# Turning the second product of a PEER expert layer: 32 sparse tokens move to the v side, gates come eight blocks at a time

## What is computed

```
s1, s2 = scores of the query halves against 128 keys each     # per token and head (8 heads)
idx, sc = the 16 best of the 128 x 128 pairs                  # expert number, score
gate = softmax(sc)
act  = gelu(u_table[idx] . h)                                 # u_table: 16384 x 1024
y    = sum over heads and experts of gate * act * v_table[idx]
```

## Time and profile before

| | us |
|---|---|
| median of 3 runs | 1489.33 (1485.82 to 1491.83) |
| profiled execution, its own time | 1488.56 |
| its span, first to last instruction | 1486.4 |
| start of the first product (chain of work) | 373.5 |
| start of `main` | 647 |
| start of `POST` | 923.5 |
| start of the second product | 960.2 |

### The profile page before, as it was taken

The page is one execution under the profiler, slowest core; times in us unless marked ns, Lnnn a source line. Parts: engine busy times, 40 slices in busy tenths (PEclk is TensorE's granted clock), DMA queues, the critical chain, the costliest instruction groups (busy, mean ns, idle before and its releaser), DMA issues.

```text
span 1486.4 us, 23381 instructions
## 1 busy us (share of the span) xinstructions
PE 1458.1 (98%) x8069; PEld 1301.4 (88%) x8069; DVE 1165.9 (78%) x2372; ACT 640.8 (43%) x1055; POOL 681.1 (46%) x394
## 2 busy tenths in 40 slices
PE   7999899999999999999999999999999999999998
PEld 6879668888999999999999999888888888888887
DVE  4747563388989999988998888578788778878876
ACT  4463472321433333467777666433332243233221
POOL 2423171233777768865545453134334434433341
PEclk9999999999999999999999999999999999999999
DMA  7400211312689999999999999699999999999993
GB/s 265 149 29 1 113 45 32 114 58 71 192 296 330 317 332 354 417 356 363 371 376 362 356 368 389 218 392 383 379 355 343 354 348 352 346 348 349 354 344 121
DMA packets 183962, 410.29 MB, mean 276 GB/s; under 512 B 12852, under 2 KB 108852, under 8 KB 182360
## 3 DMA queue, kind: packets, MB, share of 16 engines
q1 hardware_dynamic: 142296, 258.46, 49.3%
q0 software_dynamic: 41600, 151.03, 26.9%
HBM read 361.12 MB, written 48.30 MB: 275 GB/s over the span
## 4 chain that ended last, share of the span: by engine, by line
PE 75%; DVE 9%; DMA 9%; POOL 4%; issue 2%; ACT 1%; SPq 0%; DVEq 0%; ACTq 0%; POOLq 0%
PE banks L1996 17%; PE banks L1764 16%; PE banks L2065 12%; PE banks L2064 12%; PE banks L2066 12%; DMA u_rows<-in_u,idx 8%; DVE gate_rows L1623 3%; POOL u_lo L746 3%; DVE u_rows L1568 2%; POOL u_rows L762 2%; DVE u_lo L1551 1%; PE banks L1976 1%; DVE oh L1619 1%; PE banks L1791 1%; PE banks L1836 1%
## 5 line engine op out<-in xcount | busy, mean ns | idle before, releaser
L794 POOL DMA_INDIRECT v_rows<-in_v,idx x128 | 204.2, 1595 | 325.2 <-DVE x_res L1707 273.6
L2064 PE MATMUL banks<-v_hi,w_hi 128*128 128x512 f32 x768 | 298.8, 389 | 0.0
L2066 PE MATMUL banks<-v_hi,w_lo 128*128 128x512 f32 x768 | 298.8, 389 | 0.0
L2065 PE MATMUL banks<-v_lo,w_hi 128*128 128x512 f32 x768 | 298.8, 389 | 0.0
L1125 ACT ACTIVATE v_hi<-v_raw 128x1024 fp32r<-128x1024 f32 x128 | 126.3, 1050 | 326.1 <-PE banks L2066 298.5
L762 POOL DMA_INDIRECT u_rows<-in_u,idx x160 | 189.8, 1186 | 138.7 <-DVE z L1568 107.4
L1645 DVE TENSOR_TENSOR v_lo<-v_raw,v_hi 128x1024 fp32r<-128x1024 f32 x128 | 153.5, 1221 | 96.5 <-ACT v_hi L1125 96.3
L746 POOL TENSOR_TENSOR u_lo<-u_raw,u_hi 128x1024 fp32r<-128x1024 f32 x66 | 163.8, 2485 | 87.6 <-ACT u_hi L1011 53.7
L1996 PE MATMUL banks<-h_lo,u_hi 128*128 128x352 f32 x1024 | 196.1, 326 | 0.0
L1996 PE MATMUL banks<-h_hi,u_hi 128*128 128x352 f32 x1024 | 188.3, 326 | 0.0
L1996 PE MATMUL banks<-h_hi,u_lo 128*128 128x352 f32 x1024 | 184.7, 323 | 3.3 <-DVE u_lo L1551 3.3
(11 more groups left out here) (276 smaller groups left out, 2078.1 us busy)
## 6 DMA issues: line engine op xcount, KB each, us to landing
u_raw<-in_uT SPq DMA_DIRECT2D x128, 512.0 KB
v_raw<-in_v SPq DMA_DIRECT2D x128, 512.0 KB
gate_scratch<-stage SPq DMA_DIRECT2D x12, 2048.0 KB
gates<-gate_scratch SPq DMA_DIRECT2D x29, 768.0 KB
act_scratch<-act_out SPq DMA_DIRECT2D x116, 176.0 KB
act_in<-act_scratch SPq DMA_DIRECT2D x29, 704.0 KB, 7.4
wi_raw<-in_w_in SPq DMA_DIRECT2D x8, 1024.0 KB, 6.7
wq_raw<-in_w_q SPq DMA_DIRECT2D x8, 1024.0 KB, 6.0
```

Source lines behind the costliest of these rows:

```text
L794: nc.gpsimd.indirect_dma_start(v_rows[s % V_ROWS][:], None, v_flat, bass.IndirectOffsetOnAxis(ap=idx0[:, s:s + 1], axis=0)).then_inc(vg_in ...
L2064: mm(y, w, v_hi[q][:, j, ds], start=first and j == 0, stop=False)
L2065: mm(y, w, v_lo[q][j][:, ds], start=False, stop=False)
L2066: end = mm(y, w_lo[q][:, j, t * P:(t + 1) * P], v_hi[q][:, j, ds], start=False, stop=last and j == GROUP - 1)
```

## The change

1. The 32 mixed tokens leave the second product. Their v rows are gathered (32 more gathers, kind "w"), scaled by `z1 * g1` and summed by VectorE into `acc_b`; eight small float32 matmuls with `fold` add the four stacked parts into PSUM columns 0 to 31 before the last group. `g1` is loaded by four tiny DMAs. `SCALE_AT` and its transpose go.
2. Gates are built for 352 tokens: 88 batches and 11 chunks.
3. The second product is turned: TensorE holds v and streams w, 8 output tiles x 4 blocks x 3 matmuls of 352 columns. The result is y turned; at the end ScalarE copies the eight banks to `yT`, 24 TensorE transposes turn them back, and VectorE adds six tiles as before.
4. All gathers (u and v, 320) go through one order and one list of buffers. Four "w" adds lie in `POST` (`POST_ADDS`), the other 156 in groups 1 to 30 (`adds_of`, 5 or 6 per group). The first twelve v gathers share three buffers; from then on there are six.
5. Gates of the groups from 3 on are loaded for eight blocks at once (1408 KB, runs of 1024 B); activations are stored by pairs of blocks and loaded in runs of 2816 B.

```diff
-CHUNKS = ND // CHUNK
+CHUNKS = NA // CHUNK
-BATCHES = ND // BATCH
+BATCHES = NA // BATCH
+for _n in range(POST + 4, E_BLOCKS):
+    DOTS[_n] = "w" * POST_ADDS
+ALL_DOTS += "w" * (NE - ALL_DOTS.count("w")) + "v" * SLOTS
+def adds_of(g):
+    return g * ADDS_LEFT // ADD_GROUPS - (g - 1) * ADDS_LEFT // ADD_GROUPS if g <= ADD_GROUPS else 0
-Y_BANKS = (4, 5, 6, 7, 0, 1)
+Y_BANKS = (4, 5, 6, 7, 2, 3, 0, 1)
-        v_rows = [at(f"v_rows{i}", kb, [P, D]) for i, kb in enumerate((110, 114, 134, 138, 150, 154, 158, 162))]
+        WIDE, MAIN, POST_KB, LATE = (110, 114, 195, 199, 38, 42, 46, 50), (110, 114, 195, 199), (150, 110, 114), (134, 138, 177)
+        POST_TURNS = 4
+        U_LATE = U_DOTS + POST_TURNS * len(POST_KB)
...
-            def save_act(n, j):
-                sp.wait_ge(act_ready, n + 1)
+            def save_acts(i, body, pair):
+                sp.wait_ge(act_ready, i * body + (2 * pair + 2))
...
-                    sp.wait_ge(gate_staged, BATCHES)
-                    sp.dma_start(gate_d[0].rearrange("p n t -> p (n t)"),
-                                 stage[1][:].rearrange("p n t -> p (n t)")).then_inc(gate_saved[1], 16)
...
+                    if r % 2 == 0:
+                        last = isinstance(p, int) and p + KEPT + 1 == GROUPS
+                        load_pair(p * GROUP, r // 2, GROUP if last else 2 * GROUP)
...
+                if s == U_DOTS:
+                    pool.wait_ge(gate_saved[1], 16 * (CHUNKS // 2))
+                if s == U_LATE:
+                    pool.wait_ge(z_done, E_BLOCKS)
...
+            for c in range(KD):
+                act.wait_ge(y_done, c + 1)
+                copy(yT[:, c, :], ps[:, Y_BANKS[c], 0:ND]).then_inc(yT_ready, 1)
...
             weights(0, 0)
+            post_dots(POST + 4)
             split_u(POST + 5)
             split_w(0, 0)
+            post_dots(POST + 5)
             split_u(POST + 6)
+            post_dots(POST + 6)
             split_u(POST + 7)
+            post_dots(POST + 7)
...
-                for o in range(6):
+                for c in range(KD):
+                    if last and c == 6:
+                        turn(0, range(4))
+                    if last and c == 7:
+                        turn(1, (4, 5))
+                    ds = slice(c * P, (c + 1) * P)
+                    y = ps[:, Y_BANKS[c], NE:ND]
                     for j in range(GROUP):
-                        mm(y, w, v_hi[q][:, j, ds], start=first and j == 0, stop=False)
-                        mm(y, w, v_lo[q][j][:, ds], start=False, stop=False)
+                        mm(y, v_hi[q][:, j, ds], w_hi[q][:, j, :], start=first and j == 0, stop=False)
+                        mm(y, v_hi[q][:, j, ds], w_lo[q][:, j, :], start=False, stop=False)
+                        end = mm(y, v_lo[q][j][:, ds], w_hi[q][:, j, :], start=False, stop=last and j == GROUP - 1)
...
+            pe.wait_ge(dot_done, U_DOTS + NE)
+            for c in range(KD):
+                mm(ps[:, Y_BANKS[c], 0:NE], acc_b[:, c * P:(c + 1) * P], fold[:], start=False, stop=False)
             second(GROUPS - 1, 1, last=True)
```

More of the change, by code:

```diff
@@ L410, in build @@
         act_ready = sem("act_ready")
-        act_saved = [sem(f"act_saved{i}") for i in range(RING)]
+        act_saved = [sem(f"act_saved{i}") for i in range(RING // 2)]
         oh_ready = sem("oh_ready")
@@ L420, in build @@
         actg_in = [sem(f"actg_in{i}") for i in range(2)]
+        pairs_in = [sem(f"gate_pairs_in{m}") for m in range(2)]
         gates_in = [sem(f"gates_in{i}") for i in range(2)]
@@ L596, in main @@
                         save_gates(i - 1, 1)
+            sp.wait_ge(tri_ready, 2 * (TB - 1) + 1)
+            for y in range(P // NE):
+                sp.dma_start(g1[y * NE:(y + 1) * NE, :], tri[0:NE, 0, 0, y * NE:(y + 1) * NE]).then_inc(g1_in, 16)
             main(0)
@@ new lines, in second @@
+                if not isinstance(p, int) or KEPT <= p + 2 < GROUPS:
+                    load_act(p + (2 - KEPT), q)
+            for p in range(4):
+                second(p, p % 2, p)
+            with sp.Fori(1, GROUPS // 4 - 1) as i:
+                for r in range(4):
+                    second(i * 4 + r, r % 2, r)
+            for p in range(GROUPS - 4, GROUPS):
+                second(p, p % 2, p % 4)
+            sp.wait_ge(dot_done, GATHERS)
+            sp.dma_start(a["out"][0:P, :], x_res[:, 0, :]).then_inc(out_saved, 16)
@@ L679, in _ @@
+            for o in range(6):
+                half, t = o // 3, 1 + o % 3
+                ds = slice(half * 512, (half + 1) * 512)
+                sp.wait_ge(y_added, o + 1)
+                sp.dma_start(a["out"][t * P:(t + 1) * P, ds], x_res[:, t, ds]).then_inc(out_saved, 16)
+            sp.wait_ge(out_saved, 16 * 7)
         @block.gpsimd
@@ L780, in _ @@
                 s += 1
[L782 to L796, removed]
         @block.scalar
@@ L1099, in main @@
                     n = i * MAIN_BODY + (PRE + j)
-                    take_gates(i, 2 * j, first)
-                    if not (last and j == MAIN_BODY - 1):
+                    if not last or i * MAIN_BATCHES + 2 * j < BATCHES:
+                        take_gates(i, 2 * j, first)
+                    if not last or i * MAIN_BATCHES + 2 * j + 3 < BATCHES:
                         one_hot(i, 2 * j + 3)
@@ L1648, in weights @@
             def weights(g, q):
-                dve.wait_ge(gates_in[q], (g - q) * 8 + 16)
+                if g < KEPT:
+                    dve.wait_ge(gates_in[q], (g - q) * 8 + 16)
+                    gate = gates[q][:]
+                else:
+                    m, half = divmod(g - KEPT, 2)
+                    dve.wait_ge(pairs_in[m % 2], m // 2 * 16 + 16)
+                    gate = gate_pairs[m % 2][:, :, half * GROUP:(half + 1) * GROUP, :]
                 if g:
@@ L2036, in gate_matrices, with main @@
                 last.then_inc(gate_done, 1)
-            def main(i, first=False):
+            def main(i, first=False, last=False):
                 for j in range(MAIN_BODY):
@@ L2041, in main, with turn @@
                                 lambda b=b: gate_matrices(i, b, first and b < 4))
-                               for b in BATCHES_IN[j]]
+                               for b in BATCHES_IN[j] if not last or i * MAIN_BATCHES + b < BATCHES]
                     first_product(i * MAIN_BODY + (PRE + j), j, i, PRE + j, MAIN_BODY, between=between)
             main(0, True)
-            with pe.Fori(1, MAIN_TRIPS) as i:
+            with pe.Fori(1, MAIN_TRIPS - 1) as i:
                 main(i)
+            main(MAIN_TRIPS - 1, last=True)
             for n in range(POST, E_BLOCKS):
                 first_product(n, n, 0, n, 1, ring=2)
+            def turn(half, chunks):
+                for c in chunks:
+                    pe.wait_ge(yT_ready, max(c + 1, 3 * half + 3))
+                    for t in range(3):
+                        o = ps[:, Y_BANKS[3 * half + t], c % 4 * P:(c % 4 + 1) * P]
+                        end = nc.tensor.transpose(o, yT[:, c, t * P:(t + 1) * P], ident)
+                        if c % 4 == 3:
+                            end.then_inc(yT_turned, 1)
             def second(g, q, first=False, last=False):
```

223 lines of the change are left out of this document (113 added, 110 removed).

## The result

The changed kernel took 1500.1 us (median of five runs; 1494.85 to 1503.3), the kernel before 1489.33: ratio 1.0066, 95% interval 1.0047 to 1.0085. It is slower by 0.7%, where the prediction had 1473.0 and a range up to 1492. The profiled execution took 1494.85 us (span 1493.0, against 1486.4 before). "Before" and "after" stand for the two kernels from here on.

The account below looks back on a forecast made before the run. TensorE's matmuls bound the second product before, the DMA engines after. Gates -7.2, groups -4.5 and -16.2, transposes +2.9, fold +1.5, end +2, `POST` +1, buffers +4 made -16.5: median 1473 us, 8-in-10 range 1455 to 1492.

Parts of the forecast that it names:

- the stretch with a full queue is the nearer case: Second product, groups 3 to 30: DMA engines nearly keep their backlog rate, period 15.75 us against 16.33, -16.2 us.
- Both ends: Limits of a group's period in the second product: 15.2 us, equal to TensorE's, to 16.4 us, no gain.
- the third rival: Second product: DMA engines slow to the steady 349 GB/s, 18.0 us per group, time 1535; decides below 384 GB/s; chance 0.05.
- one short wait of TensorE per group: Second product, expected profile: a wait on `v_lo` or `w_lo`, about half a microsecond per group, nothing counted for the clock.
- Matmul distance: Second product: 352-column matmuls start 0.1583 us apart, 96 per group, 15.20 us against 16.33 before.
- Gates of blocks 116 to 119: First product: eight of 96 gate batches go, saving 7.2 us, with 4 as the low end.
- forecast +1, range 0 to 4: `POST`: an add before each of `split_u` 5, 6 and 7, less the removed copy, costs 1 us.
- Groups 0 to 2: Start of second product: -1.13 us per group from shorter TensorE work; three gather buffers cost a 4 us wait (0 to 10).
- Transposes and fold: End of second product: 24 transposes add 2.9 us, eight `fold` matmuls add 1.5 us.
- A share of 1, period 16.4, 1483 to 1494: Rival, second product: DMA engines give no more than a share of 1, about no change in time; chance 0.2.
- TensorE as the bound: Rival, second product: larger runs keep the backlog's rate, period 15.2 us, -31.6 instead of -16.2, time 1457; chance 0.15.
- The gather ring: Rival, second product: gathers landing after over 14.5 us starve VectorE; at 16 us, 17 us per group, time 1508; chance 0.07.

Follow-up runs that it names:

- e1_split: Changed kernel with each pair's gates loaded in two parts, chunks 0 to 5 with one group and 6 to 10 with the next: 1484.02 us, 0.9956 of before.
- f2_act1: e6_u125 with each block's activations stored by themselves, 1408 bytes a run: 1461.59 us, 0.9806 of before.
- e5_tail: e1_split with the v gathers spread anew: none in group 1, 142 over groups 2 to 31, 14 after the last group: 1465.89 us, 0.985 of before.
- e6_u125: e5_tail with the load of u block 125 issued ahead of four v loads and the gates of group 0: 1461.81 us, 0.9817 of before.
- e7_swap: e6_u125 with the split of u block 124 ahead of the first two v splits on VectorE: 1465.64 us, 0.983 of before.
- e4_turns2: Changed kernel with six buffers for v gathers from the seventh gather on (`POST_TURNS` 4 to 2): 1497.84 us, 1.0024 of before.
- f1_tail_only: Changed kernel with only the gathers moved (none in group 1, 142 over groups 2 to 31, 14 at the end), gate loads undivided: 1477.77 us, 0.9908 of before.
- b_look: The kernel before, unchanged, profiled once more: 1486.91 us.
- g1_act1: Changed kernel with each block's activations stored by themselves, nothing else: 1495.54 us, 1.0026 of before.
- e2_single: Changed kernel with gates again loaded for four blocks at a time, in runs of 512 bytes: 1494.9 us, 1.002 of before.
- e3_fewer: Changed kernel without 28 of the 32 gathers and adds of the mixed tokens, so output lacks them: 1475.69 us, 0.9877 of before.
- f3_gates1: e6_u125 with gates loaded for four blocks at a time, in runs of 512 bytes: 1469.75 us, 0.9871 of before.

## Why the prediction was wrong

**The step that failed** is "the stretch with a full queue is the nearer case", the 15.75 us per group from which the -16.2 of the sum came. The 28 groups took 457.3 us, and 455.6 without the fold (1.7), against 457.0 before: the term is -1.4. Both ends had been nearly right (16.4 above; below, 15.2 against the 15.3 to 15.5 of groups without a stall). The choice between them treated a group's 6.27 MB as one even amount of work, to be done at one rate. The runs show two things that it left out.

First, a high rate does not mean that v arrives on time. The changed kernel moves 386 GB/s, close to the 388 of the earlier trace rows, and still stalls; the forecast had 395 with short waits. The break that the third rival gave, 384 GB/s for 6.27 MB in 16.33 us, is where it came to lie, but that only says the period again: the rate is the bytes over the period. With the loads divided the engines moved 397, so 386 was no ceiling.

Second, the order in the queue. Before, 1.5 MB of gates and activations (768 and 704 KB) went ahead of each group's v; after, it is 2.1 MB and 0.7 MB in turn, and v has no stock beyond the group in either kernel. e1_split makes it 1.3 to 1.5 MB again, with the same bytes: 16 us. Before, ScalarE waited for matmuls and not for v. I had costed the gates' wide runs by their packets alone (0.8 us less per group), where they also cost a burst. The forecast's "one short wait of TensorE per group" was of the wrong kind: 17 of the 28 groups run undisturbed, and from group 0 to the end there are eight waits of 18.9 us together, the longest 4.7. I had counted nothing for the clock on the ground that the waits would be of half a microsecond. That failed with them: after the wait of 3.60 us it was 0.91 for 19 us, and over the 28 groups the matmuls at the wider distance cost the 7 us named above, beside the 16.7 us of waits. Together these are what parts the 457.3 us from the some 434 that 28 groups at 15.4 to 15.5 and the fold would take.

The Trainium skill, "DMA: Bandwidth & Descriptors", in its first table, puts the HBM side of a core at about 358 GB/s, by which a group takes 17.5 us, an estimate. The 397 GB/s over 440 us of e1_split exceed it, so on this one core it is not the limit. That the time came out slower is not its doing.

**The other terms.** Matmul distance: forecast 0.1583, measured 0.160 to 0.161 in after (0.159 in f2_act1), so a group without stalls takes 15.4 to 15.5 in after, not 15.2. It cost the sum nothing, since 15.75 was forecast, but it is what bounds e5_tail and e6_u125. Gates of blocks 116 to 119: forecast -7.2, measured -7.1. But this gain was handed back ahead of and behind it, in `main` (+5.1) and `POST` (+4.5, forecast +1, range 0 to 4). In `POST` the working looked at the adds on VectorE and not at what SyncE has in its queue. That load landed 21.51 us after issue; yet with it moved (e6_u125: 40.6 us) the stage stayed as long, and with the split moved as well (e7_swap: 39.0 us) blocks 124 to 127 took 23.8 us instead of 24.5. Its cause is only half known. In after TensorE waits 5.1 us here, twice for `u_lo` and once, 1.7 us, for ScalarE's `act_kept`, against 3.3 before, and the granted clock is 0.84 against 0.90. Groups 0 to 2: forecast +0.6 with the three buffers in it, measured +1.0, the size right and the reason wrong: with six buffers it got no better (e4_turns2), with no adds in group 1 the groups ran at 15.5 (f1_tail_only, e5_tail). The working there also adds up wrongly: 946 less 7, 36 and 5 give 980, not 983, so by its own terms the buffers came 2 us ahead of TensorE's need at 982. Transposes and fold: forecast 2.9 and 1.5, measured in groups 31 and 30 as 17.5 and 17.1 against 15.4, that is 2.1 (for 18 of the 24 transposes) and 1.7. End: +2, measured +1.6 with the other six transposes in it.

**The rivals.** "A share of 1, period 16.4, 1483 to 1494" was the nearest, though 1500 lies beyond it: period right, its waits for `v_lo` there, but with the wrong reason, since the share was 1.01 and e1_split has 1.03 with the same bytes per group. TensorE as the bound is what e5_tail and e6_u125 became. The gather ring did not starve VectorE (landing 8.6 us).

**Summed up**: forecast -16.5, measured +6.6 on the span. Of the 23.1 us between them 14.8 are the 28 groups, 5.1 `main`, 3.5 `POST`, and the rest takes back 0.3.

**What stays open.** `main`: of the twelve kernels with the change that were profiled, f2_act1 has 250.8 us from block 72 to 116 and the eleven others 253.2 to 258.7, the kernel before 252.1 and 253.0. Block by block the starts say where it goes. Blocks without a wait run at one of two paces, 5.59 or 5.77 us, in long stretches and both at a granted clock of 1.00. Before has none at 5.77 from 72 to 116, b_look three, f2_act1 six, after twenty (3.7 of the 5.1 us), e1_split 37. The rest is the net of the blocks with waits: block 115 takes 10.3 us against 6.4, two others less than before. What sets the pace is not known, and the pair stores do not: g1_act1, without them, has 38 blocks at 5.77. How much of the 4.5 us in `POST` belongs to the change, and how VectorE's load and the DMA engines' share the gain of the tail, is open too.

## What to carry to other kernels

Once the DMA engines are near full, cost a load by its place as well as by its bytes: ask how much stands in the same queue ahead of the transfer that the critical engine needs next, and how much of that is in stock. Making runs longer by loading more at once can be had without the burst, by loading half the rows of it each time. And look for the stretch where the queues are idle: in after these are the last groups, as this windows row of most of group 30 shows (DMA share 0.15). With 14 of the 160 gathers moved there and one load divided, the change that lost 0.7% gains 1.5% (e5_tail).

```profile
1452.40:1468.10 15.70, 15.70 (x100) 15.70 (x100) 8.52 (x7) 5.18 (x5) 0.00 (x0) 1.00 0.15 59
```

The fastest found are e6_u125 and f2_act1, 0.9817 and 0.9806 of the kernel before.

## What the runs showed that I had not expected

The chip moved 396 GB/s from 1000 to 1400 us (e6_u125, windows view) while TensorE did not wait once, at a DMA share of 1.03:

```profile
1000.00:1400.00 400.00, 400.00 (x2502) 400.00 (x2501) 351.19 (x282) 135.79 (x130) 188.81 (x123) 1.00 1.03 396
```

The distance of 352-column matmuls is not one number, even at full clock and without a wait. A group took 15.3 us throughout in f2_act1, 15.4 in e6_u125 and 15.5 in e5_tail, but in e7_swap 15.3 up to group 3 and 15.5 from group 6 on, so it can change within one execution. Blocks 116 to 119 of the first product took 3.8 us each in after, e1_split, e2_single, e3_fewer, e4_turns2 and e7_swap, and 4.0 in e5_tail, e6_u125, f1_tail_only, f2_act1, f3_gates1 and g1_act1.
